# Norm statistics as one-column products, spread by broadcast products, in a two-block transformer kernel

## The chip, the core and the metric

The kernel runs on 1 core of one Trainium2 chip. Its time is device microseconds from launch to end. Engines: PE (TensorE, products; PEld is its weight load), DVE (VectorE), ACT (ScalarE), POOL (GpSimd) and SP (SyncE, which issues the DMAs). TensorE runs at 2.4 GHz, or at 1.2 GHz when the granted clock is 0.5.

## The reference

The input is 512 tokens of 1024 features, fp32. A first block has two layers, each a pre-norm token mixer and a pre-norm convolutional feed-forward, with RMS norms. A second block has two layers of feed-forward, attention mixer, feed-forward, each followed by a layer norm:

```
rms:   x * rsqrt(mean(x*x) + eps) * gain
norm:  xc = x - mean(x);  xc * rsqrt(mean(xc*xc) + eps) * g + b
first block, per layer:   h = h + mixer(rms(h));  h = h + conv_ffn(rms(h));   at the end rms(h)
second block, per layer:  x = norm(alpha*x + 0.5*swiglu(x));  x = norm(alpha*x + mixers(x));
                          x = norm(alpha*x + 0.5*swiglu(x))
```

Means are taken over the 1024 features of a token. Feed-forwards are 1024 to 2 x 2816 and 2816 to 1024.

## The kernel before

Activations lie feature-major: `h[:, k, :]` holds features 128k to 128k+127 on the partitions, the 512 tokens along the free axis. There are eight feature tiles k (`KT`). Products with fp32 accuracy are made of three fp32r passes (`three`, L580 to L582): weights and activations are split in a high part (`wh`, `xh`) and a low part (`wl`, `xl`), and high*high, high*low and low*high are summed in PSUM. Weights come in chunks of two 1024-column halves: SP's DMA fills `wst`, ACT casts it to `wh` (L1411), DVE subtracts to get `wl` (L2036). Two slots alternate; a slot is refilled when `half_done` and `chunk_done` say that PE has consumed its halves.

The PSUM has two tensors of four banks, `gb` and `pm`. All queues are written out by hand, one program per engine, with semaphores between them.

There are eleven norms, numbered n: 0 for the input, 1 after mixer 0, 2 after feed-forward 0, 3 after the recurrent mixer, 4 after feed-forward 1 (the first block's final norm), then three per layer of the second block: 5 and 8 after the first feed-forward, 6 and 9 after the attention mixer, 7 and 10 after the second feed-forward. Norms 0 to 4 are RMS, 5 to 10 layer norms. Between 10 and the end there is only the output.

A norm sums over partitions, so PE does it. `sums` (L654) multiplies an all-ones 128x128 matrix with running sums of squares (`sq`), and for a layer norm with sums of `h`: five products per token half (256 tokens) for a layer norm, two for RMS. Each result stands on all 128 partitions already, in `stat` and `stat2` (`pm` banks 3 and 2). These products are plain fp32, which the trace shows as two passes each. `norm_root` on ACT (L1440) takes mean, squared mean and root over 128x256; DVE (L2043) computes the variance, subtracts the mean (`centred`), takes the reciprocal (`inverse`), scales (`scaled`), and after ACT has made `xh` subtracts to get `xl` (`low`). The feature tiles go in pairs j = 0 to 3, token halves v = 0, 1. DVE also splits the next chunk's weights between (`first`, and `split` between the two halves).

Three places of PE issue `sums`:

- `residual_out` (L681), the output product of a mixer. Its last chunk (feature tiles 6 and 7, m = 0, 1) runs by token half. In the second half `sums(n, ln_run, 0)` stands between the two tiles.
- `down_last` (L734), the last output tile of a feed-forward, by token half too. `sums` for the first half stands in the second half behind the first weight half (input tiles 0 to 5 of 22).
- `two_by_half` (L610), the first two chunks (s = 0, 1, with two output tiles m each) behind a norm. It takes pairs of input tiles as they get ready. For the first token half the two output tiles of the first chunk alternate (`together`), for the second they run one after the other (`sorted`). `sums(n, ln_run, 1)` stands behind (m 0, j 3) of the first half. Behind norms 4, 7 and 10 the second half's sums come before it (`sums(4, None, 1)`, `sums(n + 2, l, 1)`).

## Time and profile before

| | |
|---|---|
| median of 3 runs | 3489.61 us (3485.17 to 3496.29) |
| profiled execution | 3490.86 us |
| its span | 3489.1 us |
| mean granted clock | 0.983 |
| PE busy | 3355.1 us, 96% |
| PEld, DVE, ACT busy | 2769.9, 1800.8, 1408.1 us |
| HBM read | 283.61 MB, 82 GB/s |

Busy shares count an engine as working while any of its instructions is in flight; a product's duration includes its drain, so products in a row start closer together than they last. The chain of waits is followed back from the last instruction. In a timeline, brackets behind a line give the idle time of the engine ahead of it and what ended it.

### The profile page before, as it was taken

How to read it: one execution, taken by the hardware profiler on the slowest of the kernel's cores; microseconds unless marked ns; L12 is line 12 of the kernel's file. 1: busy time of each engine (PE TensorE's matmuls, PEld its weight loads, DVE VectorE, ACT ScalarE, POOL GpSimd, SP SyncE). 2: the span in 40 equal slices, each digit the busy share in tenths (PEclk: the TensorE clock that was granted, in tenths of full speed). 3: DMA queues.
4: the chain of work that ended last, by engine and by line, in shares of the span. 5: the costliest groups of instructions: out<-in, count | busy, mean ns of one | idle time of the engine just before them, and what ended most of it. 6: DMA issues, size and time to landing. Idle time of an engine off the chain costs nothing.

```text
span 3489.1 us, 46959 instructions
## 1 busy us (share of the span) xinstructions
PE 3355.1 (96%) x17468; PEld 2769.9 (79%) x17468; DVE 1800.8 (52%) x2556; ACT 1408.1 (40%) x2151; POOL 12.7 (0%) x13
## 2 busy tenths in 40 slices
PE   7999999999999999999998999999999999899997
PEld 6898888888888888888865778888888866588886
DVE  6573566538766534333586553335333567663335
ACT  5323344326544324232466442224222456542224
POOL 0000000001000000000000000000000000000000
PEclk9999999999999999999999999999999999999998
DMA  3201232322232222223210122232223211022233
GB/s 131 67 31 37 80 103 96 99 95 94 77 103 96 96 93 97 96 98 96 79 43 32 43 79 96 98 98 85 97 97 101 76 55 45 24 74 96 96 99 102
DMA packets 87432, 287.82 MB, mean 82 GB/s; under 512 B 9712, under 2 KB 11760, under 8 KB 86768
## 3 DMA queue, kind: packets, MB, share of 16 engines
q1 hardware_dynamic: 87136, 284.03, 24.6%
q8 instruction: 102, 1.67, 0.2%
q0 software_dynamic: 144, 1.71, 0.1%
q14 instruction: 50, 0.41, 0.0%
HBM read 283.61 MB, written 2.10 MB: 82 GB/s over the span
## 4 chain that ended last, share of the span: by engine, by line
PE 84%; DVE 9%; ACT 3%; issue 3%; DMA 1%; DVEq 0%; ACTq 0%; SPq 0%
PE gb L580 25%; PE gb L582 24%; PE gb L581 24%; PE gb L1250 2%; DVE wl L2036 1%; PE pm L1263 1%; PE pm L1283 1%; DMA wst<-in_weights 1%; DVE rinv L2066 1%; DVE h L2052 1%; DVE work_a L2669 1%; ACT wh L1411 1%; PE gb L1172 0%; DVE xl L2090 0%; DVE sq L2720 0%
## 5 line engine op out<-in xcount | busy, mean ns | idle before, releaser
L580 PE MATMUL gb<-xh,wh 128*128 128x512 f32 (+1 forms) x3168 | 1194.1, 377 | 54.3 <-DVE xl L2090 28.7
L582 PE MATMUL gb<-xh,wl 128*128 128x512 f32 (+1 forms) x3168 | 1171.7, 370 | 0.0
L581 PE MATMUL gb<-xl,wh 128*128 128x512 f32 (+1 forms) x3168 | 1171.4, 370 | 0.0
L2036 DVE TENSOR_TENSOR wl<-wst,wh 128x1024 fp32r<-128x1024 f32 (+2 forms) x584 | 643.6, 1115 | 445.5 <-ACT wh L1411 439.8
L1411 ACT CAST wh<-wst 128x1024 fp32r<-128x1024 f32 (+2 forms) x584 | 552.3, 960 | 603.3 <-DMA wst<-in_weights 603.2
L580 PEld LDWEIGHTS gb<-xh,wh 128*128 128x128 f32 x3168 | 608.6, 192 | 190.8 <-issue 56.2
L581 PEld LDWEIGHTS gb<-xl,wh 128*128 128x128 f32 x3168 | 608.9, 192 | 99.1 <-issue 4.9
L582 PEld LDWEIGHTS gb<-xh,wl 128*128 128x128 f32 x3168 | 608.1, 192 | 98.9
L580 PE MATMUL gb<-hid,wh 128*128 128x512 f32 (+2 forms) x1276 | 470.7, 369 | 2.0 <-DVE wl L2036 1.2
L582 PE MATMUL gb<-hid,wl 128*128 128x512 f32 (+2 forms) x1276 | 466.9, 366 | 0.0
L581 PE MATMUL gb<-hid,wh 128*128 128x512 f32 (+2 forms) x1276 | 466.9, 366 | 0.0
L2235 DVE SCALAR_TENSOR_TENSOR xf<-sq,gb 128x512 f32<-128x512 f32 x88 | 60.5, 687 | 460.4 <-ACT sq L1544 460.4
L580 PEld LDWEIGHTS gb<-hid,wh 128*128 128x128 f32 (+1 forms) x1276 | 239.8, 188 | 44.0 <-DVE wl L2036 2.4
L581 PEld LDWEIGHTS gb<-hid,wh 128*128 128x128 f32 (+1 forms) x1276 | 239.8, 188 | 40.4 <-issue 1.0
L582 PEld LDWEIGHTS gb<-hid,wl 128*128 128x128 f32 (+1 forms) x1276 | 239.8, 188 | 39.9
L1544 ACT ACTIVATE sq<-gb 128x512 f32<-128x512 f32 x88 | 52.6, 598 | 508.5 <-PE gb L582 508.4
L2238 DVE TENSOR_TENSOR hid<-xf,hid 128x512 f32 (+1 forms) x132 | 91.4, 692 | 129.5 <-ACT hid L1546 129.5
L1546 ACT CAST hid<-xf 128x512 f32 (+1 forms) x132 | 82.0, 621 | 155.2 <-DVE xf L2229 79.1
L1250 PE MATMUL gb<-work_a 32*128 32x512 f32 (+4 forms) x320 | 100.4, 620 | 15.3 <-ACT work_a L1906 8.4
L1906 ACT ACTIVATE work_a<-work_a,sm 128x512 f32<-128x512 f32 (+2 forms) x96 | 63.5, 663 | 117.8 <-DVE sm L2669 93.0
L2222 DVE SCALAR_TENSOR_TENSOR sq<-gb,prm,sq 128x511 f32<-128x511 f32 x44 | 33.0, 750 | 108.0 <-ACT sq L1537 108.0
L1537 ACT ACTIVATE sq<-gb,prm 128x512 f32<-128x512 f32 x44 | 34.2, 777 | 127.9 <-PE gb L582 127.9
(401 smaller groups left out, 2975.2 us busy)
## 6 DMA issues: line engine op xcount, KB each, us to landing
wst<-in_weights SPq DMA_DIRECT2D x408, 512.0 KB, 3.3
wst<-in_weights SPq DMA_DIRECT2D x86, 384.0 KB, 2.9
wst<-in_weights SPq DMA_DIRECT2D x84, 320.0 KB, 3.0
h<-in_x_t SPq DMA_DIRECT2D x2, 1024.0 KB, 6.3
out_t<-h SPq DMA_DIRECT2D x8, 256.0 KB, 2.3
tab<-in_first SPq DMA_DIRECT2D x1, 1984.0 KB, 15.2
tab<-in_second POOLq DMA_DIRECT2D x1, 1666.0 KB, 7.6
wst<-in_weights SPq DMA_DIRECT2D x6, 256.0 KB, 2.9
```

What stands on the lines that cost most here:

```text
L580: pe.matmul(dst, w_hi, x_hi, start=start, stop=False)
L581: pe.matmul(dst, w_hi, x_lo, start=False, stop=False)
L582: return pe.matmul(dst, w_lo, x_hi, start=False, stop=stop)
L1250: mm = pe.matmul(gb[:, score_banks(s) + i, 0:(k1 - k0) * P], lhs[:, qt * P:(qt + 1) * P], rhs[:, k0 * P:k1 * P], start=True, stop=True)
L1263: mm = pe.transpose(pm[:, i, j * P:(j + 1) * P], src[:, j * P:(j + 1) * P], IDENT)
L1411: act.copy(wh[:, s, m, 0:cols], wst[:, s, m, 0:cols]).then_inc(hi_split, 1)
L1544: act.activation(gate, gb[:, 2 * s, :], ACT.Silu).then_inc(up_act, 1)
L1546: act.copy(hid[:, 0, bass.ds(j, 1), :], val.unsqueeze(1)).then_inc(hid_hi, 1)
L1906: ins = act.activation(e_slot(s, i)[:, 0:w], src, ACT.Exp, bias=small[:, i:i + 1], scale=-1.0 if kind in BIASED else 1.0, accum_out=small[ ...
L2036: dve.tensor_tensor(wl[:, s, m, a], wst[:, s, m, a], f32(wh[:, s, m, a]), ALU.subtract).then_inc(lo_split, 1)
L2235: dve.scalar_tensor_tensor(val, gate, 0.5, gb[:, 2 * s + 1, :], ALU.mult, ALU.mult).then_inc(group_free, 1)
L2238: dve.tensor_tensor(hid[:, 1, bass.ds(j, 1), :], val.unsqueeze(1), f32(hid[:, 0, bass.ds(j, 1), :]), ALU.subtract).then_inc(hid_lo, 1)
```

## The change

Statistics: the data are now the stationary operand and a unit column the moving one, so a sum over partitions comes out on the token's partition. One PSUM tile of 128x4 holds a half: two columns of sums, two of sums of squares, one for each block of 128 tokens. DVE and ACT work on two columns (`small_stat`). A mean or an inverse is then spread over all partitions by a product of the broadcast column with the identity, into `mean_of` (`pm` bank 2) or `inv_of` (`pm` bank 3), which both halves share; `centred` and `scaled` read them there.

Places: in `residual_out` the sums are issued inside the second token half's first tile, and DVE's order there is other (a square tile of its own, `slot(30)`, for tile 5 and the tail). `variance(1)` goes ahead of `split`. In `two_by_half` both token halves alternate the two output tiles.

```
+        def stat_of(v):
+            return pm[:, 0 if v else 3, 0:4]
+        def unit(i):
+            return units[:, 3 - i:7 - i]
+        mean_of, inv_of = pm[:, 2, 0:T // 2], pm[:, 3, 0:T // 2]
...
             def two_by_half(c, n, ln_run, out_=False):
...
-                    for m, j in sorted(together) if v else together:
+                    for m, j in together:
                         two_tiles(v, 0, m, j)
                         if v == 0 and m == 0 and j == 3 and not isinstance(ln_run, str):
-                            sums(n, ln_run, 1)
+                            sums(n, ln_run, 1, out_)
                     for m in range(2):
                         for j in range(KT // 2):
                             two_tiles(v, 1, m, j)
+                            if v == 0 and m == 0 and j == 1 and ln_run is not None:
+                                spread_mean(n, 1)
+                            if v == 0 and m == 0 and j == 3:
+                                spread_inverse(n, 1)
...
+            def column(v, kind, src, first, last):
+                for b in range(2):
+                    t = slice(2 * P * v + P * b, 2 * P * v + P * b + P)
+                    mm = pe.matmul(stat_of(v), src[:, t], unit(2 * kind + b), start=first and b == 0, stop=last and b == 1)
+                return mm
+            def first_sums(n, ln_run, v):
+                if ln_run is not None:
+                    pe.wait_ge(h_added, 2 * (n - 5) + 2)
-                    pe.matmul(stat[:, t], ONES, xf[:, 0, t], start=True, stop=False)
+                    column(v, 0, xf[:, 0, :], True, False)
                     pe.wait_ge(h_tail[v], 2 * (n - 1) + 1)
+                    column(v, 0, h[:, 6, :], False, False)
+            def last_sums(n, ln_run, v, out_=False):
                 pe.wait_ge(tail_added, 2 * n + v + 1)
+                column(v, 1, sq[:, 0, :], ln_run is None, False)
                 if ln_run is not None:
                     pe.wait_ge(h_tail[v], 2 * (n - 1) + 2)
+                    column(v, 0, h[:, 7, :], False, False)
                 pe.wait_ge(tail_sq[v], 2 * n + 2)
+                column(v, 1, last_square(out_), False, True).then_inc(sq_summed, 1)
+            def over_all(dst, v, i):
+                for b in range(2):
+                    mm = pe.matmul(dst[:, b * P:(b + 1) * P], small_stat(v, i)[:, b:b + 1].broadcast_to([P, P]), IDENT, start=True, stop=True)
+                return mm
+            def spread_mean(n, v):
+                pe.wait_ge(mean_ready, 2 * (n - 4) + v + 1)
+                over_all(mean_of, v, MEAN).then_inc(mean_spread, 1)
+            def spread_inverse(n, v):
+                pe.wait_ge(rinv_ready, 2 * n + v + 1)
+                over_all(inv_of, v, INV).then_inc(inv_spread, 1)
...  in residual_out, last chunk
+                            if v == 1 and m == 0 and k == 0:
+                                first_sums(n, ln_run, 0)
+                            elif v == 1 and m == 0 and k == 4:
+                                last_sums(n, ln_run, 0, True)
+                            elif v == 1 and m == 1 and k == 1:
+                                spread_inverse(n, 0)
                         if v == 1:
                             mm.then_inc(chunk_done if m else half_done, 1)
-                            if m == 0:
-                                sums(n, ln_run, 0)
+                            if m == 0 and ln_run is not None:
+                                spread_mean(n, 0)
...  in down_last
+                                    if v == 1 and f == DOWN[0] + 2 and ln_run is not None:
+                                        spread_mean(n, 0)
+                                    elif v == 1 and f == HALF and ln_run is not None:
+                                        spread_inverse(n, 0)
+                                    elif v == 1 and f == DOWN[0] + 4 and ln_run is None:
+                                        if isinstance(n, int) and n == 4:
+                                            spread_mean(n, 0)
+                                        spread_inverse(n, 0)
...  ACT, norm_root of a layer norm
-                    act.activation(xf[:, 0, t], stat[:, t], ACT.Square, scale=1.0 / D).then_inc(d2_ready, 1)
-                    act.mul(mu2[:, t], stat[:, t], 1.0 / D).then_inc(mean_ready, 1)
-                    act.activation(rt[:, t], rt[:, t], ACT.Sqrt, bias=eps_of[EPS_LN]).then_inc(rt_ready, 1)
+                    act.activation(small_stat(v, ROOT), small_stat(v, VAR), ACT.Sqrt, bias=eps_of[EPS_LN]).then_inc(rt_ready, 1)
...  DVE, norm
                         dve.wait_ge(sq_summed, 2 * n + v + 1)
+                        dve.tensor_scalar(small_stat(v, MEAN), stat_of(v)[:, 0:2], 1.0 / D, None, ALU.mult).then_inc(mean_ready, 1)
+                        dve.tensor_tensor(small_stat(v, MEAN2), small_stat(v, MEAN), small_stat(v, MEAN), ALU.mult).then_inc(d2_ready, 1)
-                        dve.scalar_tensor_tensor(rt[:, t], stat2[:, t], 1.0 / D, xf[:, 0, t], ALU.mult, ALU.subtract).then_inc(var_ready, 1)
-                        centred(0, v)
+                        dve.scalar_tensor_tensor(small_stat(v, VAR), stat_of(v)[:, 2:4], 1.0 / D, small_stat(v, MEAN2),
+                                                 ALU.mult, ALU.subtract).then_inc(var_ready, 1)
...
-                    dve.reciprocal(rinv[:, t], rt[:, t]).then_inc(rinv_ready, 1)
+                    dve.reciprocal(small_stat(v, INV), small_stat(v, ROOT)).then_inc(rinv_ready, 1)
+                    centred(0, v)
...
-                    dve.tensor_tensor(dst, two(j, v), over_tiles(rinv[:, t], 2), ALU.mult).then_inc(xf_ready, 1)
+                    dve.tensor_tensor(dst, two(j, v), over_tiles(inv_of, 2), ALU.mult).then_inc(xf_ready, 1)
...
                 half(0)
+                variance(1)
                 if split:
                     split()
-                variance(1)
                 inverse(1)
...  DVE, residual_out
-                for m in (4, 5):
-                    add_squares(n, m)
-                for m in range(2):
-                    dve.wait_ge(S("out_half"), ...)
-                    tail_residual(n, 6 + m, 0, out_tail(m, 0), ln)
-                    if m == 0:
-                        tail_add(n, 0)
+                dve.wait_ge(S("out_half"), halves + 1)
+                tail_residual(n, 6, 0, out_tail(0, 0), ln)
+                if ln is not None:
+                    sum_of_two(n)
+                add_squares(n, 4)
+                dve.wait_ge(S("out_half"), halves + 2)
+                tail_residual(n, 7, 0, out_tail(1, 0), ln)
+                add_squares(n, 5, True)
+                tail_add(n, 0)
...  PE, main program
+            pe.wait_ge(S("ones_ready"), 1)
             sums(0, None, 0)
+            spread_inverse(0, 0)
...
+            spread_mean(3 * LAYERS + 4, 1)
+            spread_inverse(3 * LAYERS + 4, 1)
```

## Rows read from the trace of the kernel before

**Rows 1.** The chain that ended last, share of the span by line (page, part 4).

```profile
PE gb L580 25%; PE gb L582 24%; PE gb L581 24%; PE gb L1250 2%; DVE wl L2036 1%; PE pm L1263 1%; PE pm L1283 1%; DMA wst<-in_weights 1%; DVE rinv L2066 1%; DVE h L2052 1%; DVE work_a L2669 1%; ACT wh L1411 1%; PE gb L1172 0%; DVE xl L2090 0%; DVE sq L2720 0%
```

**Rows 2.** Waits of PE: line, waited for, us in total, times, longest us.

```profile
PE gb L580 <- DVE xl L2090: 28.7, 25, 4.0
PE gb L580 <- DVE xl L2093: 16.4, 7, 5.6
```

**Rows 3.** Timeline of PE at n = 6: start us, us, engine, line, operation, times [idle].

```profile
2002.36 0.60 PE L665 MATMUL pm<-xf,com 128*128 128x256 f32 x2
2004.09 0.59 PE L674 MATMUL pm<-sq,com 128*128 128x256 f32 x2
...
2011.57 0.38 PE L580 MATMUL gb<-xh,wh 128*128 128x256 f32 x1 [4.02 <-DVE xl L2090]
...
2022.23 0.59 PE L674 MATMUL pm<-sq,com 128*128 128x256 f32 x2
```

**Rows 4.** Timeline of PE in mixer 0: one-column products, a broadcast spread.

```profile
75.31 3.63 PE L812 MATMUL pm<-com,work_a 128*128 128x1 f32 x32
...
85.98 1.95 PE L828 MATMUL pm<-com,sm 128*128 128x128 f32 x16
```

**Rows 5.** Groups of instructions by form: times, busy us, mean ns, idle before.

```profile
L2066 DVE RECIPROCAL rinv<-rt 128x256 f32<-128x256 f32 x22 | 38.6, 1753 | 18.8 <-ACT rt L1445 18.8
...
L2147 DVE TENSOR_TENSOR h<-gb,h 128x512 f32<-128x512 f32 x36 | 24.1, 688 | 63.2 <-PE gb L582 63.2
...
L2695 DVE RECIPROCAL sm<-sm 128x2 f32<-128x2 f32 x48 | 7.6, 159 | 1.6 <-ACT work_a L1906 1.0
...
L1711 ACT ACTIVATE sm<-pm,eps_a 128x16 f32<-128x16 f32 x3 | 0.8, 274 | 1.6 <-PE pm L812 1.6
```

**Rows 6.** Timeline of DVE at n = 6: first scaling of each token half.

```profile
2007.67 0.69 DVE L2083 TENSOR_TENSOR h<-h,rinv 128x512 f32<-128x512 f32 x1
...
2025.80 0.69 DVE L2083 TENSOR_TENSOR h<-h,rinv 128x512 f32<-128x512 f32 x1
```

**Rows 7.** Timeline of PE at n = 6, second half: first and third of three waits.

```profile
2030.98 0.39 PE L580 MATMUL gb<-xh,wh 128*128 128x256 f32 x1 [0.25 <-DVE xl L2090]
...
2034.82 0.38 PE L580 MATMUL gb<-xh,wh 128*128 128x256 f32 x1 [0.94 <-DVE xl L2090]
```

**Rows 8.** Stretches: us, busy (instructions) of PE, PEld, DVE, ACT, POOL; PEclk; DMA; GB/s.

```profile
80.00:83.30 3.30, 3.30 (x9) 2.58 (x9) 3.19 (x4) 1.71 (x5) 0.00 (x0) 0.51 0.00 0
95.40:99.00 3.60, 3.60 (x36) 3.60 (x34) 3.33 (x6) 2.33 (x3) 0.00 (x0) 1.00 0.26 97
1688.00:1694.30 6.30, 5.85 (x23) 5.49 (x24) 3.44 (x4) 3.44 (x5) 0.00 (x0) 0.50 0.00 1
2022.60:2031.00 8.40, 8.15 (x69) 7.92 (x67) 7.40 (x11) 4.97 (x11) 0.00 (x0) 1.00 0.00 0
```

**Rows 9.** Timeline at n = 1: last statistic, first scaling of each half.

```profile
412.07 0.59 PE L674 MATMUL pm<-sq,com 128*128 128x256 f32 x2
...
415.00 0.69 DVE L2083 TENSOR_TENSOR xf<-h,rinv 128x512 f32<-128x512 f32 x1
...
429.59 0.69 DVE L2083 TENSOR_TENSOR xf<-h,rinv 128x512 f32<-128x512 f32 x1
```

**Rows 10.** Timeline of ACT at n = 2: the next weight split.

```profile
783.03 1.05 ACT L1411 CAST wh<-wst 128x1024 fp32r<-128x1024 f32 x1 [1.97 <-DMA wst<-in_weights]
```

**Rows 11.** Timeline at n = 7: PE's return, first scaling of the second half.

```profile
2393.47 0.58 PE L580 MATMUL gb<-xh,wh 128*128 128x256 f32 x1 [3.50 <-issue]
...
2400.81 0.69 DVE L2083 TENSOR_TENSOR h<-h,rinv 128x512 f32<-128x512 f32 x1
```

**Rows 12.** Timeline at n = 2: last low part, next statistic product.

```profile
791.56 0.88 DVE L2093 SCALAR_TENSOR_TENSOR xl<-xf,prm,xh 128x256 fp32r<-128x256 f32 x2 [0.18 <-ACT xh L1466]
...
794.89 0.38 PE L669 MATMUL pm<-sq,com 128*128 128x256 f32 x1
```

More of the change, by code:

```diff
@@ L1416, in split_hi, with square @@
                     split_half(c, s, m, cols[m])
-            def square(n, m, src):
+            def square(n, m, src, out_=False):
+                if m == 5 and out_:
+                    act.activation(last_square(out_), src, ACT.Square).then_inc(sq_ready, 1)
+                    return
                 if m >= 2:
@@ L2126, in add_squares @@
                     dve.wait_ge(sq_added, 5 * n + m - 1)
-                dve.tensor_tensor(sq[:, 0, :], sq[:, 0, :], sq[:, 1, :], ALU.add).then_inc(sq_added, 1)
+                dve.tensor_tensor(sq[:, 0, :], sq[:, 0, :], last_square(out_ and m == 5), ALU.add).then_inc(sq_added, 1)
             def tail_add(n, v):
```

98 lines of the change are left out of this document (51 added, 47 removed).

## The prediction

> **What bounds the kernel now.** I read the chain of waits first: the three lines of TensorE's (PE's) three-term products hold 73% of it [rows 1]. Only three things shorten the run: fewer or shorter passes on PE, shorter waits of PE, or more time at its higher clock. The table of waits sizes the second: 28.7 us in 25 waits and 16.4 us in 7 waits, all for `xl`, the low part of a normed activation [rows 2]. They sit at the eleven norms (numbered n = 0 to 10 in the text above), where all later work needs the norm. A large one comes after a token mixer of the second block: last statistic product at 2004.09, next product at 2011.57 after 4.02 us idle [rows 3]. The third is visible in the stretches: 2.4 GHz normally, 1.2 GHz (0.50) for 6.30 us after such waits [rows 8]. The change touches only the norms, so everything between them is taken as unchanged.
>
> **Statistic products.** A product of ones over 256 tokens is two passes; four products take 2004.09 - 2002.36 = 1.73 us, 0.43 each [rows 3]. Each becomes two column products of 128 tokens, two passes each. 32 one-column passes took 3.63 us [rows 4], 0.11 a pass, so 0.44 per old product: no gain, no loss. The layer-norm statistics of one token half stay at about 2.2 us, the RMS ones at 0.87.
>
> **Spreading.** New on PE: a spread is two products over 128 columns, four passes. 16 such passes took 1.95 us [rows 4], so 0.5 us each. RMS norms get one per half, layer norms two. Those behind which PE would have waited anyway are free; the others lengthen PE's stream.
>
> **Statistics on ScalarE and VectorE.** Reciprocal on 128x256 costs 1.753 us and on 128x2 0.159 us [rows 5], the largest single saving, 1.6 us per half. The two activations and the root on 128x256 become three VectorE instructions and a root on two columns. The nearest rows are 0.16 us (the small reciprocal) and 0.27 us (a root from PSUM, 16 columns) [rows 5]. With hand-overs I take 1.25 us from last column product to inverse for layer norm, 0.75 for RMS. Bounds: 0.9 (no hand-over) and 1.8 (each handed over at 0.2).
>
> **Full-width operands now in PSUM.** Subtracting the mean and scaling read `pm` in place of SBUF. The row of a 128x512 add with a PSUM operand shows 688 ns [rows 5]; the scaling from SBUF shows 0.69 us [rows 6]. So I charge nothing. The Trainium skill, page "Perfetto Trace Analysis", section "Optimizing Scalar/DVE Operations", speaks against this: it gives a VectorE instruction about 60 ns of access on SBUF and about 125 ns on PSUM. By that, eight such instructions a half would add 0.5 us to a layer norm half, some 6 us in all; the rows show no such difference, and the sum leaves it out.
>
> **First token half after a mixer (n = 1, 3, 6, 9).** The products now stand inside the last quarter instead of behind it. At n = 6 before: last statistic ends at 2004.09 + 0.43 = 2004.52, scaling starts 2007.67, 3.15 later [rows 3, 6]. A three-term pass over 256 tokens takes 8.15/69 = 0.119 us [rows 8], so one input tile (three passes) takes 0.36 and the quarter of eight 2.87; it began at 2002.36 - 2.87 = 1999.49. After: one tile, the first two sums (0.87), four tiles (1.43), the last three (1.31) end at 2003.46. Then three tiles (1.07), mean spread (0.5), two tiles (0.72), inverse spread (0.5), some 0.2 to drain: scaling starts at 2006.47, 1.2 us earlier. The inverse has been waiting since 2004.7, so PE's place is what is late. At n = 1 the same working: last statistic ends 0.87 + 5 tiles into the quarter, at 411.43 instead of 412.50; then three tiles, two tiles and a spread put scaling at 413.93 against 415.00 [rows 9], 1.07 earlier. VectorE's new order (tail add, sum of two, square adds) delivers 0.2 to 0.7 us before PE asks; if that slack is wrong, PE waits by as much. Gain: 2 x 1.2 + 2 x 1.07 = 4.5 us.
>
> **First half after a feed-forward (n = 2, 4, 5, 7, 8, 10).** The products stay where they were. Layer norm: three tiles, spread, three tiles, spread, drain put scaling at +3.35 against +3.15: 0.2 us later, for n = 5, 8. At n = 2, 4, 7 another thing ends last: ScalarE's weight split waits 1.97 us for a DMA and starts at 783.03 [rows 10], and the norm's own activation is queued behind it. Nothing lost or won. n = 0: PE idles, root and reciprocal gain 1.8 us, spread at the low clock and hand-overs take 1.3: -0.5.
>
> **Second token half (all but n = 10).** Here the place of the spreads costs. Its statistics are multiplied after six of the eight groups of the first chunk (a group is 6 passes, 0.72 us). The mean spread then stands four groups later, the inverse spread six: it shares its bank with the first half's inverse. At n = 6 before: statistic ends 2022.23 + 0.43 = 2022.66 and scaling starts 2025.80, +3.14 [rows 3, 6]. After: VectorE does the variance ahead of the second weight split, so it waits for PE and the split ends at about +2.0, while PE wants it at +1.43: 0.55 wait. Inverse spread begins +5.4, scaling +6.1: 3.0 later. PE arrives for the second half at +8.8 instead of +7.2. From scaling to first `xl` it takes 3.2 and then 1.93 per pair of tiles (waits at 2030.98 and 2034.82 are two pairs apart, 3.84 [rows 7]): pairs at +9.3, 11.2, 13.2, 15.1. Before, sorted order left three waits of 0.25 to 0.95 us [rows 7] and finished the first chunk at +15.75. Now other tile's groups fill waits, but the last pair comes at +15.1 and three groups follow: +17.2. Loss 1.45 us, at n = 5, 6, 8, 9: 5.8. RMS: scaling was at 429.59 [rows 9] with no wait afterwards; it moves by 2.3 us, the spread adds 0.5, one wait of 0.7 is left: +1.3 at n = 0, 1, 2, 3: 5.2. n = 7: PE returns at 2393.47 after 3.50 us that no engine caused [rows 11] and scaling ran at 2400.81, long before PE needed it; now it waits for twelve groups (8.6 us) and both spreads, some of them at the low clock, until about 2405.3. Of these 4.5 us 1.7 were slack: loss 2.8. n = 4, with PE back earlier and a shorter RMS chain, 0.5. The second half's new order also frees the first tile's weight buffer two groups (1.4 us) later; the next chunk is first read at least eight groups on, which covers it, and 1.4 us at each of nine norms would be the price without that cover.
>
> **End (n = 10).** Nothing queues on PE. 0.2 later in the first half, 1.6 less reciprocal, 0.5 for a spread: -0.85.
>
> Sum without the clock: -4.5 + 0.4 - 0.5 + 5.8 + 5.2 + 2.8 + 0.5 - 0.85 = +8.9 us.
>
> **The clock.** The granted clock falls after idle stretches. At n = 2 the last `xl` pair was done at 791.56 + 0.88 = 792.44, the last group needs 0.72, yet the products began at 794.89 [rows 12]: 1.7 us lost. At n = 5 and 8, 5.85 us busy at 0.50 [rows 8] is 2.9 us of work, and a second fall follows in the second half. After: first waits shrink (n = 1, 3 by 1.5 us, scaling 1.07 earlier and PE 0.5 longer; n = 5, 8 by 0.8, PE 1.0 longer and scaling 0.2 later; n = 2 by the 0.5 of its spread) and those of the second half are spread out. Of about 13 us really lost I give back 9: 1.7 at n = 2, 1.6 at n = 1 and 3 together, 3.2 each at n = 5 and 8, less 0.4 at n = 6 and 9.
>
> Against it: PE had been busy without a gap in a run of 32 one-column passes [rows 4], and the clock still was 0.51 just behind it, in 80.00 to 83.30; behind another such run, 95.40 to 99.00, it stayed 1.00 [rows 8]. So columns do not hold the clock surely. The Trainium skill, page "TensorE: Matmul & The Clock Gate", section "What's actually happening", says the gate follows how busy the array has been recently; by the first run, the array hardly counts as busy in such products; the second shows no fall. The layer-norm statistics now are 20 such passes each, 2.2 us in a row in eight places where PE is pressed (first half at n = 5, 7, 8, 10, second at n = 5, 6, 8, 9). I give each a chance of 0.4, between the one run that was followed by a fall and the one that was not and shorter than both, and a price of 1.8 us, about what n = 2 loses: +5.8.
>
> Total 8.9 - 9 + 5.8 = +5.7 us on the profiled execution's 3490.86 (its span 3489.1 and 1.8 around it), itself 1.25 above the median of 3489.61. So 3495 against that median.
>
> **Rivals.** (a) Faster: the late place of the second half's spreads costs nothing, because waits of its `xl` are filled with the second tile's groups, and the clock stays up. For it: three waits of that kind at n = 6 [rows 7] and a reciprocal of 1.75 gone. Against: PE's order puts six groups ahead. Sum: 8.9 - 14.3 (all second-half losses out) - 9 = -14.4: 3475. (b) Slower: one-column statistics drop the clock at every layer norm, in both halves, from the point where they are 2.2 us in a row. All eight places at 1.8 are 14.4 instead of 5.8, and half of the 9 isn't given back: 5.7 + 8.6 + 4.5 = +18.8, 3508. For it stands the fall behind a stretch without idle time, against it the run with none. The page's rule on the clock, named above, points this way. (c) Nothing moves: gains and losses stay inside waits that `xl` sets by VectorE's pace (1.93 us a pair, untouched): 3490.
>
> **How the numbers follow.** 0.3%, 10.5 us, is about what a measurement of this kernel tells from no change. Chances: forecast 0.46 (its own range 3489 to 3503, 0.06 of it above the bound), (a) 0.16, (b) 0.24, (c) 0.14. Faster 0.16, within 0.54, slower 0.30. The likeliest time is (forecast's) 3495. The range from 3477 to 3512 reaches (a) within 2 us, takes in (b), and covers the bounds of the hand-overs (0.35 less to 0.55 more in some 18 halves, half of them hidden: -3 to +5); it leaves about two in ten outside.
>
> **What would show it.** At n = 6 the first half's statistics end before the quarter's first output tile does, and the first `xl` wait is near 2 us instead of 4.02. At n = 6 second half: first scaling 6 us behind its statistic, and a new wait of PE on `wl`. At n = 7 the second half's scaling waits for a spread. Clock: 1.00 at n = 2, and 0.50 just behind column products with no idle time ahead. I am wrong if PE does not wait in the second half, if columns take over 0.15 us a pass, or if granted clock falls nowhere near a norm.

## The result, and the profile after

| | before | after |
|---|---|---|
| median (8 runs each, same chip) | 3491.01 us (3481.18 to 3498.67) | 3506.17 us (3504.09 to 3513.79) |
| ratio of the runs | | 1.0056, 95% interval 1.0042 to 1.0071 |
| profiled execution's span | 3489.1 us | 3502.3 us |
| PE busy | 3355.1 us, 17468 instructions | 3375.3 us, 17772 |
| DVE, ACT busy | 1800.8, 1408.1 us | 1765.1, 1395.2 us |

The change makes the kernel slower by half a per cent; this lies outside the 0.3% that the prediction called no change. The page's table of engines, after:

```profile
PE 3375.3 (96%) x17772; PEld 2789.7 (80%) x17772; DVE 1765.1 (50%) x2585; ACT 1395.2 (40%) x2127; POOL 12.7 (0%) x13
```

VectorE has 36 us less to do, and it buys nothing: PE, which bounds the kernel, has 20 us more. PE's waits after, the same table as [rows 2]:

```profile
PE gb L602 <- DVE xl L2163: 27.9, 36, 3.3
PE gb L602 <- DVE xl L2166: 15.1, 13, 3.3
...
PE gb L602 <- DVE xf L2315: 4.0, 2, 2.1
```

The longest wait is shorter (at n = 6 1.87 us where 4.02 was), but 36 and 13 waits stand where 25 and 7 stood, 43.0 us in all where 45.1 were: little time was removed, most was cut in pieces. The last row is new.

First half at n = 6, PE and then VectorE, against [rows 3, 6]:

```profile
2004.92 0.59 PE L684 MATMUL pm<-units,h 128*128 128x4 f32 x4
2005.37 0.59 PE L684 MATMUL pm<-units,work_a 128*128 128x4 f32 x4
2006.97 0.60 PE L713 MATMUL pm<-com,st 128*128 128x128 f32 x4
2008.13 0.61 PE L713 MATMUL pm<-com,st 128*128 128x128 f32 x4
2012.76 0.38 PE L602 MATMUL gb<-xh,wh 128*128 128x256 f32 x1 [1.87 <-DVE xl L2163]
```

```profile
2006.00 0.16 DVE L2127 TENSOR_SCALAR st<-pm 128x2 f32<-128x2 f32 x1 [2.34 <-PE pm L684]
2006.91 0.17 DVE L2138 RECIPROCAL st<-st 128x2 f32<-128x2 f32 x1 [0.36 <-ACT st L1521]
...
2008.87 0.69 DVE L2156 TENSOR_TENSOR h<-h,pm 128x512 f32<-128x512 f32 x1 [0.56 <-PE pm L713]
```

The rows show that the moving operand of a statistic product is 128x4, four columns of which one is ones and the rest zero, and not one column. The inverse is there 1.3 us after the last column product (before: 3.15 to the scaling), and then waits 1.0 us for its turn in PE's queue. The second half, PE and VectorE, against [rows 6, 7]:

```profile
2023.71 0.59 PE L684 MATMUL pm<-units,work_a 128*128 128x4 f32 x4
2028.62 0.60 PE L713 MATMUL pm<-com,st 128*128 128x128 f32 x4
2030.49 0.60 PE L713 MATMUL pm<-com,st 128*128 128x128 f32 x4
2034.47 0.39 PE L602 MATMUL gb<-xh,wh 128*128 128x256 f32 x1 [0.50 <-DVE xl L2163]
2036.39 0.39 PE L602 MATMUL gb<-xh,wh 128*128 128x256 f32 x1 [0.95 <-DVE xl L2163]
2038.31 0.39 PE L602 MATMUL gb<-xh,wh 128*128 128x256 f32 x1 [0.22 <-DVE xl L2163]
2040.21 0.38 PE L602 MATMUL gb<-xh,wh 128*128 128x256 f32 x1 [0.21 <-DVE xl L2163]
```

```profile
2027.13 0.15 DVE L2138 RECIPROCAL st<-st 128x2 f32<-128x2 f32 x1
...
2031.22 0.69 DVE L2156 TENSOR_TENSOR h<-h,pm 128x512 f32<-128x512 f32 x1 [1.28 <-PE pm L713]
```

The inverse is ready at 2027.3 and used at 2031.2: 3.9 us in which it waits for the groups ahead of its spread. Scaling comes 7.1 us behind the last statistic; it was 3.1. Of the 7.1 us 1.0 belongs to the clock: right behind the columns it fell, though PE had not been idle.

```profile
2021.40:2024.60 3.20, 3.20 (x31) 3.20 (x29) 0.23 (x2) 0.00 (x0) 0.00 (x0) 1.00 0.00 0
2024.60:2028.00 3.40, 3.40 (x19) 3.40 (x18) 2.65 (x5) 0.29 (x1) 0.00 (x0) 0.50 0.01 2
```

Where it did not fall (n = 5, 8 and 9, and n = 6 in a second profile) the scaling comes 6.1 us behind.

What one spread costs PE's stream, at n = 0: from the last product ahead of it to the second behind it.

```profile
31.42 0.28 PE L604 MATMUL gb<-xh,wl 128*128 128x256 f32 x1
31.54 0.60 PE L713 MATMUL pm<-com,st 128*128 128x128 f32 x4
31.90 0.36 PE L602 MATMUL gb<-xh,wh 128*128 128x256 f32 x1
32.10 0.28 PE L603 MATMUL gb<-xl,wh 128*128 128x256 f32 x1
```

32.10 - 31.42 = 0.68, less two products at their pitch of 0.12: 0.44 us. It is 0.44 in all places where PE did not wait for the spread's data and the clock was at 2.4 GHz, and 1.04 where the clock is low (1680.72, 2766). The same reckoning gives a layer norm half's statistics 2.16 before and 2.23 after, an RMS half's 0.87 and 0.90. There are 36 spreads, two each half for layer norms and for n = 4, one else; 32 lie ahead of n = 10. So 32 x 0.44 + 2 x 0.6 + 11 x 0.07 + 10 x 0.04 = 16.5 us more work in PE's stream before n = 10. PE's busy time in the stretch up to there (3.00 to 3446.00 before, to 3460.00 after) grew by that:

```profile
3.00:3460.00 3457.00, 3350.97 (x17583) 2766.28 (x17584) 1739.78 (x2534) 1372.92 (x2089) 12.47 (x9) 0.99 0.24 82
```

```profile
3.00:3446.00 3443.00, 3334.32 (x17316) 2750.58 (x17317) 1772.23 (x2512) 1384.17 (x2110) 12.51 (x9) 0.99 0.25 82
```

The waits of PE in it, added up, went from 111.2 to 108.4 us. 16.7 - 2.8 = 13.9, and n = 10 starts 14.2 us later. The end gives 1.0 back.

### The profile page after: what moved, and what is told of

Its sections match the earlier page's. It is cut to its first block, busy times and chain, and to the rows that moved or that the text cites. A ratio compares the mean times of both kernels' runs of the same rounds, so it can differ in the third digit from the quotient of the medians.

```text
span 3502.3 us, 47561 instructions
## 1 busy us (share of the span) xinstructions
PE 3375.3 (96%) x17772; PEld 2789.7 (80%) x17772; DVE 1765.1 (50%) x2585; ACT 1395.2 (40%) x2127; POOL 12.7 (0%) x13
## 4 chain that ended last, share of the span: by engine, by line
PE 84%; DVE 9%; ACT 3%; issue 3%; DMA 1%; DVEq 0%; ACTq 0%; SPq 0%
PE gb L602 24%; PE gb L603 24%; PE gb L604 24%; PE gb L1314 2%; DVE wl L2105 2%; PE pm L1327 1%; PE pm L1347 1%; DMA wst<-in_weights 1%; PE pm L684 1%; DVE work_a L2749 1%; ACT wh L1479 1%; DVE xl L2163 1%; PE pm L713 0%; DVE h L2121 0%; ACT work_a L1975 0%
## 5 line engine op out<-in xcount | busy, mean ns | idle before, releaser
L602 PE MATMUL gb<-xh,wh 128*128 128x512 f32 (+1 forms) x3168 | 1193.1, 377 | 54.6 <-DVE xl L2163 27.9
```

The costliest lines, as they stand in the source:

```text
L602: pe.matmul(dst, w_hi, x_hi, start=start, stop=False)
```

## The experiments

Each was timed in 5 rounds (the last in 3) beside the kernel before. The medians stand beside ratios to the kernel before in the same rounds; the two differ by some us, and the intervals reach 3 to 9 us to each side, so a few us between two kernels say little. "Waits" are all of PE's ahead of n = 10, "low" is the time at 1.2 GHz ahead of n = 10 by the trace's clock records, both of one profiled execution. "Mixers" is the part of "low" in the two mixers of the second block (1733 to 1990 and 2812 to 3070 in the kernel before, the same products in the others), where no edit changes an instruction; "rest" is what remains.

| kernel | median us | ratio to before, interval | waits | low | mixers | rest |
|---|---|---|---|---|---|---|
| before | 3487 to 3493 | 1 | 111.2 | 102.4 | 27.3 | 75.1 |
| after | 3506.17 | 1.0056 (1.0042 to 1.0071) | 108.4 | 88.7 | 37.5 | 51.2 |
| after, again | 3505.06 | 1.0043 (1.0027 to 1.0060) | 110.0 | 85.3 | 41.0 | 44.3 |
| after, sorted | 3521.27 | 1.0087 (1.0072 to 1.0103) | 108.3 | 119.5 | 51.2 | 68.3 |
| the same again | 3522.81 | 1.0093 (1.0068 to 1.0118) | 109.1 | 126.3 | 41.0 | 85.3 |
| after, early spreads | 3498.81 | 1.0020 (1.0009 to 1.0032) | 99.9 | 105.8 | 54.6 | 51.2 |
| early and sorted | 3496.14 | 1.0017 (1.0004 to 1.0031) | 100.9 | 109.2 | 27.3 | 81.9 |
| after, statistics behind the tile | 3515.92 | 1.0074 (1.0059 to 1.0089) | 113.3 | 109.2 | 27.3 | 81.9 |
| after, spreads twice | 3527.13 | 1.0103 (1.0081 to 1.0125) | 107.9 | 99.0 | 34.1 | 64.9 |
| before, together | 3492.86 | 1.0000 (0.9990 to 1.0009) | 104.5 | 119.5 | 54.6 | 64.9 |
| before, inside | 3483.72 | 0.9984 (0.9974 to 0.9994) | 104.5 | 99.0 | 44.4 | 54.6 |
| before, inside and together | 3478.16 | 0.9966 (0.9953 to 0.9979) | 103.6 | 88.7 | 41.0 | 47.7 |
| before, dummy columns | 3512.69 | 1.0065 (1.0047 to 1.0082) | 107.6 | 105.8 | 27.3 | 78.5 |
| before, dummy dense | 3514.93 | 1.0071 (1.0053 to 1.0089) | 110.8 | 102.4 | 30.7 | 71.7 |

The mixers' share of the low time runs from 27.3 to 54.6 us, and their time from 514 to 525 us, with nothing changed in them; one mixer alone moved by 3 to 4.5 us between two profiles of one kernel. So totals of one profile say little of an edit, and "rest" is the column to compare.

"Token-major" below names the changed form, in which sums come out on the token's partition and are spread by products. Two theories went in. Theory 1: the second half loses by where spreads and groups stand. Theory 2: one-column products let TensorE's clock fall.

**The second half's order put back.**

```
-                    for m, j in together:
+                    for m, j in sorted(together) if v else together:
```

> The changed kernel, with the second token half's order of the first two output tiles put back (one after the other). Theory 1 (places: the second half is late because of where spreads and groups stand, and the alternating order frees the first tile's weight buffer two groups later): the new waits of PE on the first up-projection's activation at n = 4 (2.11 us) and n = 7 (1.94) go, -4; at n = 5, 6, 8, 9 the late xl pairs now are waited for with nothing between, +1.5 each, +6; sum +2, about 3508. Theory 2 (clock: one-column products let the granted clock fall, the order is nothing): within 2 us of 3506, both waits shorter or not. If the order alone made the change slow, it would be 3500 or less.

Measured 3521.27, 15 us above the changed kernel (11 to 17 by the ratios of the two runs of each), against the 2 that theory 1 gave; theory 2 expected no change. The two waits on the first up-projection are gone, as expected, and all waits together are the same (108.3 against 108.4). What is more is PE's busy time for the same 17772 instructions:

```profile
PE 3391.6 (96%) x17772; PEld 2803.6 (80%) x17772; DVE 1766.0 (50%) x2585; ACT 1396.2 (40%) x2127; POOL 12.7 (0%) x13
```

16.3 us more than the 3375.3 of the changed kernel, with 31 us more at the low clock. Whether that was this execution's or the order's, the same kernel once more had to tell.

> The changed kernel with the second half's two output tiles one after the other, once more and unchanged. Its first profile had no more waiting than the changed kernel (115.9 against 116.1 us in all), but 119.5 us at the low clock ahead of n = 10 against 88.7 and 85.3. If that belongs to the order (waits with nothing between leave PE idle where the clock is judged), the second profile has over 105 us at the low clock too; if it was the execution's, some 85 to 100, and the time stays 15 us over the changed kernel for a reason that the trace of one execution does not show.

Low for 126.3 us, PE busy 3392.6, median 3522.81. It belongs to the order, in this kernel: the waits are equal, and outside the untouched mixers the sorted order has 68.3 and 85.3 us at the low clock, the alternating order 51.2 and 44.3. The same sign stands in the other pairs below (before 75.1 against together 64.9, inside 54.6 against inside and together 47.7, early and sorted 81.9 against early 51.2), but there the times differ by 0 to 6 us and not always the same way. What in the order lets the clock fall, no run here isolates.

**The second half's spreads early.**

```
+                    if v == 0 and ln_run is not None:
+                        spread_mean(n, 1)
                     for m in range(2):
                         for j in range(KT // 2):
                             two_tiles(v, 1, m, j)
-                            if v == 0 and m == 0 and j == 1 and ln_run is not None:
-                                spread_mean(n, 1)
-                            if v == 0 and m == 0 and j == 3:
+                            if v == 0 and m == 0 and j == 1:
                                 spread_inverse(n, 1)
```

> The changed kernel, with the second half's two spreads earlier in PE's order: the mean before the second chunk's groups (was behind two of them), the inverse behind two (was behind four). The scaling of the second half then starts 1.4 us earlier after norms whose statistics stand inside the groups. Theory 1 (late spreads): -1.4 at each of n = 5, 6, 8, 9, -1.5 at n = 7, -0.5 at n = 0 to 3: about -9, 3497. Theory 2 (clock): the same number of column products at the same places, so the low stretches stay and the time is 3504 to 3508.

3498.81, 7 us less by the medians and 8 to 13 by the ratios; the forecast of theory 1 was 9. Second half at n = 6, VectorE and then PE:

```profile
2029.13 0.69 DVE L2156 TENSOR_TENSOR h<-h,pm 128x512 f32<-128x512 f32 x1 [0.52 <-PE pm L713]
```

```profile
2034.30 0.38 PE L602 MATMUL gb<-xh,wh 128*128 128x256 f32 x1 [0.27 <-DVE xl L2163]
2036.22 0.39 PE L602 MATMUL gb<-xh,wh 128*128 128x256 f32 x1 [0.24 <-DVE xl L2163]
2038.12 0.39 PE L602 MATMUL gb<-xh,wh 128*128 128x256 f32 x1 [0.21 <-DVE xl L2163]
```

The scaling stands 4.2 us behind its statistic in place of 6.1 (7.1 where the clock fell), and three waits of 0.2 to 0.3 are left of four with 1.9 us. So the late place cost some 7 of the 15 us. The rest has another cause.

**Early and sorted.** (The two diffs above together.)

> The changed kernel with the second half's spreads early (3499 alone) and the second half's two output tiles one after the other (3521 alone). If the order of the tiles costs because it meets the late low parts, its price grows with how late they are: 0 with the timing of the kernel before (scaling 3.1 us behind the statistic), 15 us with the changed kernel (6 to 7 us behind), and between them here (some 5 us behind): +5 to +9 over the early spreads alone, 3504 to 3508. If the order costs 15 us by itself in the token-major form, 3514.

Neither: 3496.14, the same as early alone. By its place the scaling would stand 4.2 us behind the statistic; in the profile it is 5.7 at n = 5, 6, 8 and 9, because the clock fell right behind the columns there. The order of the tiles costs 11 to 17 us with the late spreads and nothing with the early ones. Why it does not grow evenly with the delay stays open.

**One part alone: together on the kernel before.**

```
-                    for m, j in sorted(together) if v else together:
+                    for m, j in together:
```

> The kernel before, with one part of the change alone: the two output tiles of the first chunk alternate in the second token half too. Theory 1: PE's waits on xl in the second half (2.1 us in three waits at n = 6) are filled by the other tile's groups, -1 at each of n = 5, 6, 8, 9; the buffer of the first tile is free 1.4 us later, and at n = 4 and 7 PE gets a new wait on the first up-projection's activation of about 2 us each: sum about 0, 3488 to 3494, with those two waits in the trace. Theory 2 (order is nothing, clock is all): the same time, but no such waits.

No change in time, as expected, and 6.7 us less waiting; but the waits at n = 4 and 7 that theory 1 wanted are not there. They need the late low parts as well as the order. The profile has 17 us more at the low clock in spite of the order; they lie in the untouched mixers, which took 10 us longer in it.

**The mixer part undone.**

```
-                            if v == 1 and m == 0 and k == 0:
-                                first_sums(n, ln_run, 0)
-                            elif v == 1 and m == 0 and k == 4:
-                                last_sums(n, ln_run, 0, True)
-                            elif v == 1 and m == 1 and k == 1:
+                            if v == 1 and m == 1 and k == 2 and ln_run is not None:
+                                spread_mean(n, 0)
+                            elif v == 1 and m == 1 and k == 5:
                                 spread_inverse(n, 0)
...
-                            if m == 0 and ln_run is not None:
-                                spread_mean(n, 0)
+                            if m == 0:
+                                sums(n, ln_run, 0, True)
```

> The changed kernel, with the first half's statistics after a mixer put back behind the last quarter's first output tile, and their spreads three input tiles apart behind them (the orders of the other engines stay). The forecast's step for this part was -1.2 us at n = 6, 9 and -1.07 at n = 1, 3: undone it costs 4.5 us, 3511. Theory 2: the statistics again are followed by an idle PE, so the clock is low after them, and it costs more than 4.5: 3514. If the part was worth nothing: 3506.

+9.7 us by the medians and 6 to 11 by the ratios, more than the 4.5 expected: waits are 4.9 us longer, and outside the mixers the clock is low for 31 us more. This part of the change is a gain.

**The clock: dummy column products against dense ones, in the kernel before.** In `sums` of a layer norm, ahead of the first product:

```
+                    for _ in range(10):
+                        pe.matmul(stat[:, 256 - 256 * v:257 - 256 * v], IDENT, ONES[:, 0:1], start=True, stop=True)
...  the other kernel
+                    for _ in range(5):
+                        pe.matmul(stat[:, HV[1 - v]], ONES, com[:, 0:256], start=True, stop=True)
```

> The kernel before, with ten one-column products on constants (20 passes, nobody reads them) ahead of the statistics of each layer norm half, twelve places. Their time is 2.2 us a place by the rows of one-column passes (0.11 a pass), 26 us if none is hidden by a wait. Theory 2 (clock: column products let the granted clock fall): on top of that a low stretch behind many of them, 1.7 us each where PE is pressed, eight places, so 10 us or more over the kernel with dense products: 3525 against 3515. Theory 1 (places): the same time as with dense products, within 3 us.

> The kernel before, with five products of ones over 256 columns (10 passes, constants, nobody reads them) at the same twelve places as the one-column products of the companion kernel: 2.2 us a place too, 26 us in all if nothing hides them, so about 3517. Both theories: no new low stretch of the clock behind them, rather fewer than before. Theory 2: some 10 us faster than the companion; theory 1: equal to it within 3 us.

3512.69 with columns, 3514.93 with dense products: the intervals lie over each other. Both took the same time in the queue, columns first:

```profile
2388.95 2.29 PE L666 MATMUL pm<-com 128*128 128x1 f32 x20
2391.10 0.68 PE L667 MATMUL pm<-xf,com 128*128 128x256 f32 x2
```

```profile
1673.87 2.32 PE L666 MATMUL pm<-com 128*128 128x256 f32 x10
1676.03 0.59 PE L667 MATMUL pm<-xf,com 128*128 128x256 f32 x2
```

2.15 and 2.16 us, and 105.8 against 102.4 us at the low clock. In sum, columns cost this kernel no more than dense products. But the clock does not fall in the same places. Behind the columns it falls at once, with PE busy all the time, at n = 5 and n = 6 like this (first fence); behind the dense products it does not (second, n = 5):

```profile
1678.81:1682.40 3.59, 3.59 (x11) 2.88 (x11) 0.00 (x0) 0.17 (x1) 0.00 (x0) 0.56 0.33 119
2010.30:2013.70 3.40, 3.40 (x10) 2.68 (x9) 0.00 (x0) 0.65 (x2) 0.00 (x0) 0.50 0.09 35
```

```profile
1676.03:1682.00 5.97, 5.97 (x43) 5.71 (x42) 3.42 (x5) 2.10 (x4) 0.00 (x0) 1.00 0.30 95
```

I count as such a fall one that has 20 passes of columns in the 4 us ahead of it and no idle time of PE in the 8 us ahead. The kernel with dummy columns has it at 5 of 12 layer norm halves (the first ones of n = 5, 6, 8, 9 and 10). In the one with dense products every fall at a norm has idle time of PE in the 8 us ahead. The eight profiles of token-major kernels have 21 in 96 halves: after 3 (n = 5 and 8 first, n = 6 second), after again 0, the others 2 to 5. The five profiles without column products at the norms have no fall without such idle time at any of their 60 halves.

So theory 2 is right that one-column products let the clock fall, and wrong that this made the change slow: the changed kernel has less time at the low clock than the kernel before (88.7 and 85.3 against 102.4 us, without the mixers 51.2 and 44.3 against 75.1), and the pair of dummies differs by 2 us the other way. With dummy columns the low time around n = 5 to 9 is 37.5 us, 13.7 of them directly behind columns; with dense ones it is 41.0, all behind waits. In sum the falls behind columns did not come on top of the others.

**One part alone: the statistics inside the quarter, still by ones.** The kernel before, with the changed VectorE and ScalarE order of `residual_out` and the tile `slot(30)`, and on PE:

```
+                            if v == 1 and m == 0 and k == 0:
+                                first_sums(n, ln_run, 0)
+                            elif v == 1 and m == 0 and k == 4:
+                                last_sums(n, ln_run, 0, True)
...  the products in both as before
+                pe.matmul(bank[:, t], ONES, last_square(out_)[:, t], start=False, stop=True).then_inc(sq_summed, 1)
```

> The kernel before, with one part of the change alone: the statistics after a mixer are issued inside the last quarter's first output tile, with VectorE's and ScalarE's new order and the square tile of its own, but still as products of ones over 256 tokens, so with no spread. Theory 1 (places): the statistics end 1.06 to 1.8 us earlier at n = 1, 3, 6, 9 and the scaling follows them by the old 3.15 us: -1.1 to -1.8 each, -4 to -7 in all, 3484 to 3488, and nothing of the losses in the second halves. Rival: the gain of this part needs the short chain on two columns (the inverse ready 1.25 us behind the statistics), so this alone is worth under 2 us: 3490 to 3493.

3483.72, ratio 0.9984: the gain of theory 1, 3.3 us by the medians and 5.6 by the ratio, without any spread. At n = 6 the first wait is 2.94 us (4.02 before, 1.87 with the short chain on two columns), and the sum of waits is 6.7 us less at no more PE work.

**The changed kernel again.**

> The changed kernel once more, unchanged, for a second profiled execution. If the low stretches of the clock in the mixers belong to the code, they stand at the same places (17 us of 0.50 at 2994, 6.8 us at 1908); if they depend on the execution, they stand elsewhere, and the differences of up to 5 us that a stretch of the second block's mixer shows between two profiles say nothing about the change. Time 3504 to 3508 either way.

The changed kernel took 3505.06. The 1.2 GHz stretches in the second block's mixers did move between two executions of the same kernel, here 1904 to 1926 and 2989 to 3016, first execution and then second (the last three columns are granted clock, DMA share, GB/s):

```profile
2989.00:3016.00 27.00, 24.50 (x114) 14.96 (x112) 17.64 (x56) 13.02 (x37) 0.00 (x0) 0.68 0.06 20
1904.00:1926.00 22.00, 18.80 (x111) 10.46 (x109) 17.01 (x55) 13.15 (x37) 0.00 (x0) 0.84 0.07 25
```

```profile
2989.00:3016.00 27.00, 22.45 (x139) 14.01 (x138) 20.39 (x58) 15.88 (x43) 0.00 (x0) 0.81 0.06 20
1904.00:1926.00 22.00, 20.01 (x91) 12.76 (x89) 14.38 (x45) 9.01 (x25) 0.00 (x0) 0.61 0.07 25
```

0.68 and 0.84 in one, 0.81 and 0.61 in the other. The untouched mixer of the first second-block layer thus ran 0.7 us faster than before in one profile and 3.6 slower in the other; the second layer's 3.7 and 0.7 slower. Such a difference between two profiles is not the change.

**Every spread twice.**

```
-                for b in range(2):
+                for b in (0, 1, 0, 1):
                     mm = pe.matmul(dst[:, b * P:(b + 1) * P], small_stat(v, i)[:, b:b + 1].broadcast_to([P, P]), ...)
```

> The changed kernel, with each spread product issued twice (four products, eight passes, in place of two and four): 34 spreads, 30 of them ahead of n = 10. Theory A: a spread stands in PE's stream, and no wait gets shorter for it; then the second copy costs its full 0.5 us, 30 times, +14 to +16, 3520. Theory B (the forecast's: spreads behind which PE waits anyway are free, and the loss comes from their late place): the copy is hidden at n = 0 to 3 and after the mixers, and costs some 5 us, 3511.

3527.13, 21 us more by the medians, 16 by the ratios. There are 36 spreads (the expectation said 34). A pair now takes twice the 0.44, at n = 0:

```profile
33.57 1.05 PE L713 MATMUL pm<-com,st 128*128 128x128 f32 x8
34.37 0.36 PE L602 MATMUL gb<-xh,wh 128*128 128x256 f32 x1
```

34.37 - 33.57 = 0.80 where one copy took 0.36, so the copy costs 0.44, and 36 x 0.44 = 16. The profile's PE is busy 24.2 us longer (3399.5); the 8 us beyond the copies go with 10 us more at the low clock. Theory A holds: spreads are paid in full, and no wait hides them. The waits (107.9) did not shrink.

**The two parts without a spread.** (The diffs of "together" and "inside".)

> The kernel before, with the two parts of the change that need no spread: statistics after a mixer inside the last quarter (products of ones), and both output tiles of the first chunk alternating in both halves. If the parts add up as they measured alone (-4.5 and 0 us): 3484 to 3486. If the alternating order fills the three waits of 2.1 us at n = 4, 5, 6, 8, 9 that the first part left (1.4 us less in each trace at n = 5, 6, 8, 9): another 3 to 6 us less, 3478 to 3483. If it brings a new wait on the first up-projection's activation as in the changed kernel, 3487 or more.

3478.16, ratio 0.9966: 0.3% faster than before, and 0.8% faster than the change by the medians. It is the best version here. Its waits on `xl`:

```profile
PE gb L586 <- DVE xl L2114: 19.8, 22, 2.9
PE gb L586 <- DVE xl L2117: 15.5, 8, 5.6
```

Against it the token-major kernel with early spreads, which has these two parts as well, takes 20.6 us more (3498.81). The two profiled executions differ by 18.4 us: 16.5 are the work in PE's stream worked out above, the waits are 3.7 us shorter, and the second block's mixers, with no instruction changed, took 5.1 us longer; 0.5 are left. The account of the change is then: 12 us won by the two parts, 19 to 21 lost by the token-major form with its spreads early, of which 16.5 are work in PE's queue, and some 7 more lost by the late place of the spreads.

## Why the prediction was right, and where its sum was wrong

The time lay in the range, at 3506 close to rival (b)'s 3508, but for another reason than (b) gives. The forecast's 3495 was 11 us low, and slower by more than 0.3% had a chance of 0.30 only. That the range held is partly luck: its upper end stood at 3512 to take in (b). Its steps without the columns' 5.8 sum to -0.5 (its total has 8.9 - 9 = -0.1, since the parts of the clock term add up to 9.3 and not 9), and 13 to 14 were measured. Step by step: the start of the same PE instruction in both traces gives an offset, and a stretch has added what the offset grew by in it (first the first profile of the changed kernel, then the second).

| stretch | forecast | measured |
|---|---|---|
| n = 0 | +0.8 | +0.5, +0.6 |
| n = 1, 3 | -0.6 each | +0.6, +0.8 and -1.0, -1.0 |
| n = 2 | -0.4 | +1.5, +0.9 |
| n = 4 | +0.5 | +2.8, +4.7 |
| n = 5, 8 | -1.55 each | 0.0, -1.3 and +0.4, -1.2 |
| n = 6, 9 | +0.45 each | +1.7, +0.3 and +0.2, +0.2 |
| n = 7 | +2.8 | +5.6, +5.9 (and 1.7 just behind it) |
| end | -0.85 | -1.0, -1.0 |
| falls behind columns | +5.8 | some 4.4, 0 (in the rows of n = 5, 6 and 8) |
| untouched mixers | 0 | +1.5, +3.1 |

**First halves after a mixer** were right: the statistics end inside the quarter, the scaling is set by PE's place for the spread, the inverse is there 1.3 us behind the last column product (1.25 forecast), the first wait is 1.87. The size, 4.5 us, is about right: 3.3 and 5.6 us (medians, ratios) when added alone, 9.7 and 6.3 when undone.

**Price of a spread**: 0.5 forecast, 0.44 measured. Of the column products, which move four columns each and not one: no gain, no loss forecast, +0.07 and +0.04 a half measured. Operands in PSUM: nothing charged, and the row agrees, 686 ns against 0.69 us from SBUF [rows 6].

```profile
L2156 DVE TENSOR_TENSOR h<-h,pm 128x512 f32<-128x512 f32 x56 | 38.3, 686 | 20.6 <-PE pm L713 19.3
```

**What failed first is the sentence "those behind which PE would have waited anyway are free".** In sum none was; at n = 0 alone PE idles ahead of the first spread. A spread stands between groups that PE can do, and it stands ahead of the scaling that sets the wait, so the wait moves with it. Doubling the spreads cost 16 to 21 us and shortened no wait.

**n = 4 and n = 7** were mis-sized, 3.3 forecast in all and 8.4 to 12.3 measured. Part of it is the step "the first tile's weight buffer is free two groups later, which covers it". It isn't covered: PE waits for the first up-projection's activation, at n = 4 and n = 7 (neither wait stood before).

```profile
1343.60 0.49 PE L602 MATMUL gb<-xh,wh 128*128 128x512 f32 x1 [2.11 <-DVE xf L2315]
...
2429.06 0.49 PE L602 MATMUL gb<-xh,wh 128*128 128x512 f32 x1 [1.94 <-DVE xf L2315]
```

ScalarE must first split the weights that refill this buffer, and its activation is queued behind that split and a table load of 1.28 us:

```profile
1339.78 1.05 ACT L1479 CAST wh<-wst 128x1024 fp32r<-128x1024 f32 x1 [7.25 <-DMA wst<-in_weights]
...
2425.24 1.05 ACT L1479 CAST wh<-wst 128x1024 fp32r<-128x1024 f32 x1 [7.06 <-DMA wst<-in_weights]
2426.31 1.28 ACT L1613 ACT_TABLE_LOAD   x1
```

I had looked at when the buffer is read next by PE, and not at what stands behind the split in ScalarE's queue. (The same load stood there before, at 2415.58, and PE did not wait there.) The transfer also lands late: issued at 2420.11 it takes 5.1 us, the one behind it (2421.53) 5.0; at n = 6, issued at 2041.36, 3.2. With the alternating order two transfers are issued 1.43 us apart, 2.87 before; but in "inside and together" they are too (2404.46 and 2405.89), and the first lands in 3.2. Why they run side by side at n = 4 and 7 of the token-major kernels alone stays open. Early spreads leave both waits (1.3 and 2.2 us); sorting removes them and costs more by the clock.

**The second halves** were right in mechanism: scaling forecast 6.1 us behind the statistic, 6.1 measured at n = 5, 8 and 9 and 7.1 at n = 6, where the clock fell; the new wait on `wl` 0.30 us (0.55 forecast) at n = 5, 8 and 9; RMS waits of 0.53 at n = 0 to 3 (0.7 forecast). Early spreads give back 7 us of what the place costs.

**The clock** term was right in both mechanisms and wrong in what they add up to. Falls behind columns: a chance of 0.4 at eight places and 1.8 us each were forecast. The first profile has three, at n = 5 like this, and the second none:

```profile
1668.00:1679.90 11.90, 11.90 (x103) 11.90 (x103) 3.25 (x9) 1.77 (x4) 0.00 (x0) 1.00 0.19 56
1679.90:1683.30 3.40, 3.40 (x19) 3.40 (x18) 0.88 (x3) 1.34 (x2) 0.00 (x0) 0.50 0.17 63
```

Their price can be read in the table, where the profiles differ by 1.3, 1.5 and 1.6 us at n = 5, 6 and 8. The other side, the 9 us given back, arrived too: around n = 5 PE has 1.9 us more to do and is busy 1.7 us less in the second profile, with no low clock left (before, then changed kernel, the same products at the ends).

```profile
1660.00:1733.00 73.00, 66.96 (x465) 62.20 (x464) 40.50 (x68) 35.14 (x61) 0.00 (x0) 0.93 0.21 68
1664.91:1736.65 71.74, 65.30 (x501) 60.79 (x500) 37.55 (x72) 33.02 (x57) 0.00 (x0) 1.00 0.22 70
```

That is 3.6 us given back, for 3.2 forecast; n = 8 gave 3.5, n = 1 and 3 together 3.6 (1.6 forecast), n = 2 0.6 (1.7). What the prediction left out is that the clock would be low elsewhere: around n = 4 and 7 for 10.2 us before and 10.2 and 20.5 after, and in the second block's mixers for 27.3 us before and 37.5 and 41.0 after. The part in the mixers moves between executions, as the table of runs shows. Over the whole stretch PE's busy time grew by just the work added. The two profiles agree within 1 us in time although one has three falls behind columns and the other none, so no time of the whole kernel shows a price for them.

One reading in the prediction is off: the stretch 95.40 to 99.00 is the second run of 32 passes itself, not what follows it. Behind it, in 99.00 to 103.00, the granted clock was 1.00 in the kernel before, so the argument stands there; but it was 0.57 in the same stretch of the changed kernel, and in 12 of the 14 profiles a fall begins in this second run or just behind it.

The Trainium skill, page "TensorE: Matmul & The Clock Gate", section "What's actually happening", has the gate follow how busy the array was recently. I had read into it that one-column products hardly count as busy. The traces agree with that reading: 21 falls in 96 halves and 5 in 12 behind such products with PE in work all the time, none in 60 behind dense ones.

**Rival (a)**, that waits are filled by the second tile's groups and the clock stays up, is true of the waits under the order alone (104.5 us on the kernel before, 111.2 without it), and even that bought no time (ratio 1.0000). It is not true of the change.

## What to carry to other kernels

Where one engine bounds the kernel, a change that takes 36 us from another engine and puts 16 on the bounding one loses, even if each chain of dependences gets shorter: count first what is added to the bounding queue, in full, and only then what waits may become shorter. A small product that spreads a value has its place in an in-order queue; its value is late by the groups ahead of it. If a change has several parts, time them apart: here two of them, taken without the third, beat both kernels. Before a difference of two profiles is read as an edit's, take a second profile of one kernel: here mixers that no edit touched moved by 3 to 4.5 us each.

## What the runs showed of the hardware

- A one-column fp32 pass takes as long in the queue as a 4-column or a 128-column one: 20 one-column passes 2.15 us, 20 four-column passes 2.15, and a spread of four 128-column passes 0.44, 0.11 each; a 256-column pass takes 0.216.
- The clock can fall with PE never idle, right behind 20 passes of one or four columns: at 5 of 12 places with ten dummy one-column products, at 21 of 96 with the changed statistics, and at none of 60 with dense ones. In the rows above it is at 0.50 for 3.4 us then. In no profile does it fall with PE in work for the 8 us before at any other place than behind such passes or the mixer's runs of some 30 one-column ones.
- PE at 1.2 GHz takes 1.04 us for a spread instead of 0.44.
- Equal waits, other clock: sorted groups had 108.3 and 109.1 us of waits, alternating ones 108.4 and 110.0, but 68.3 and 85.3 against 51.2 and 44.3 us at 1.2 GHz outside the second block's mixers, and 16 us more of busy time.
- Two untouched mixers took from 514 to 525 us in 14 profiles, with 27 to 55 us at 1.2 GHz.
- A reciprocal on 128x2 in place of 128x256 is 0.16 us against 1.753 [rows 5].
- Two transfers of 512 KB issued 1.43 us apart landed after 3.2 and 4.2 us in one kernel, and after 5.1 and 5.0 us in another.
